# Attention over cached pages moved into the units of the forgetting attention

## The reference, cut to what matters

```python
qc, kc, vc = [t.astype(f32).reshape(B, L, H_C, HEAD_DIM) for t in jnp.split(qkv_c, 3, axis=-1)]
logf = jax.nn.log_sigmoid(f_raw.astype(f32) + P['fox_f_bias'][l].astype(f32))
if fox_past is None:            # the prompt
    k_all, v_all, lf_all = kc, vc, logf
else:                           # the samples: cached pages first, then the own 8 tokens
    k_all = jnp.concatenate([pk.astype(f32), kc], axis=1)
    v_all = jnp.concatenate([pv.astype(f32), vc], axis=1)
    lf_all = jnp.concatenate([plf.astype(f32), logf], axis=1)
d_all = jnp.cumsum(lf_all, axis=1)
# per head: s = q.k/sqrt(d) + D_t - D_s, masked to s <= t, softmax over the keys, p @ v
oc = forgetting_attention(qc, k_all, v_all, d_all[:, -L:], d_all, qpos, kpos)
```

## Time and profile before

| what | us |
|---|---|
| median of 3 runs | 1983.02 (1982.95 to 1983.48) |
| the profiled execution's own time | 1979.1 |
| its span | 1977.1 |
| forgetting attention, first to last instruction | 497.2 to 642.0 |
| attention over cached pages | 642.7 to 741.7 |
| delta rule, first instruction | 742.5 |

### The profile page before, as it was taken

One profiled execution on the slowest core, in us unless ns is written; L12 is line 12 of the kernel. 1 busy time (PEld: TensorE's weight loads), 2 busy tenths in 40 slices (PEclk: granted clock), 3 DMA queues, 4 the chain that ended last, 5 costly groups with the idle time before them and its releaser, 6 DMA issues. The chain is left out here.

```text
span 1977.1 us, 27253 instructions
## 1 busy us (share of the span) xinstructions
PE 1736.5 (88%) x10093; PEld 1499.7 (76%) x10099; DVE 857.0 (43%) x1427; ACT 572.4 (29%) x928; POOL 507.5 (26%) x710
## 2 busy tenths in 40 slices
PE   6789988999788577779869799999999998999997
PEld 2557876899565236669848599999999998778876
DVE  1451007630565223345434435555555554445444
ACT  2421132321444013222223323333333332232322
POOL 0531012220000102776303333333333332111111
PEclk6899988999899768889879899999999999999999
DMA  8325531221200217733142121111111110544443
GB/s 309 122 79 168 171 101 68 78 78 39 73 1 1 68 61 201 166 85 90 52 154 86 54 73 45 50 43 42 42 42 42 42 42 20 163 158 150 152 156 127
DMA packets 120189, 182.73 MB, mean 92 GB/s; under 512 B 31228, under 2 KB 88652, under 8 KB 116786
## 3 DMA queue, kind: packets, MB, share of 16 engines
q1 hardware_dynamic: 117650, 172.80, 27.8%
q10 hardware_dynamic: 2464, 8.91, 1.2%
HBM read 150.91 MB, written 30.65 MB: 92 GB/s over the span
## 5 line engine op out<-in xcount | busy, mean ns | idle before, releaser
L2279 PE MATMUL fu_ps<-h_hi,fu_whi 128*128 128x364 f32 (+1 forms) x1056 | 233.9, 330 | 12.4 <-ACT fu_whi L2327 12.4
L2279 PE MATMUL fu_ps<-h_lo,fu_whi 128*128 128x364 f32 (+1 forms) x1056 | 233.7, 330 | 0.0
L2279 PEld LDWEIGHTS fu_ps<-h_hi,fu_whi 128*128 128x128 f32 x1056 | 183.9, 189 | 12.5 <-ACT fu_whi L2327 12.5
L2279 PEld LDWEIGHTS fu_ps<-h_lo,fu_whi 128*128 128x128 f32 x1056 | 183.9, 189 | 0.0
L2284 PE MATMUL fu_ps<-h_hi,fu_wlo 128*128 128x364 f32 (+1 forms) x1056 | 183.1, 329 | 0.0
L2284 PEld LDWEIGHTS fu_ps<-h_hi,fu_wlo 128*128 128x128 f32 x1056 | 176.9, 188 | 0.0
L2500 PE MATMUL fd_ps<-fd_whi,fd_yhi 128*128 128x512 f32 x396 | 124.3, 395 | 19.5 <-DVE fd_wlo L2554 16.1
L2297 POOL TENSOR_TENSOR fu_wlo<-fu_w,fu_whi 128x1024 fp32r<-128x1024 f32 x44 | 117.6, 2673 | 86.1 <-ACT fu_whi L2327 86.1
L2333 ACT ACTIVATE fu_zp<-fu_ps 128x728 f32<-128x728 f32 x44 | 34.3, 779 | 356.2 <-PE fu_ps L2284 356.2
L2525 ACT ACTIVATE fd_whi<-fd_w 128x1024 fp32r<-128x1024 f32 x66 | 69.9, 1060 | 207.7 <-PE fd_ps L2500 182.9
L2500 PE MATMUL fd_ps<-fd_wlo,fd_yhi 128*128 128x512 f32 x396 | 123.7, 394 | 0.0
(11 more groups left out here) (320 smaller groups left out, 3254.0 us busy)
## 6 DMA issues: line engine op xcount, KB each, us to landing
fd_w<-in_w_down SPq DMA_DIRECT2D x66, 512.0 KB, 3.6
wa<-in_w_ada SPq DMA_DIRECT2D x24, 1024.0 KB, 7.2
fu_w<-in_w_up SPq DMA_DIRECT2D x44, 512.0 KB, 3.6
fp_w<-in_w_fm SPq DMA_DIRECT2D x16, 512.0 KB, 3.3
scr_la<-dr_la SPq DMA_DIRECT2D x16, 384.0 KB, 4.0
dr_la<-scr_la SPq DMA_DIRECT2D x16, 384.0 KB, 5.5
scr_qkv<-fp_y SPq DMA_DIRECT2D x9, 544.0 KB, 2.7
dr_stg<-scr_qkv SPq DMA_DIRECT2D x8, 576.0 KB, 6.0
```

The costliest lines, as they stand in the source:

```text
L2279: pe.matmul(ps[slot][:, n, 0:size], w_hi[:, slot, kk, :], h[:, kk, c:c + size], start=(kk == 0 and h is K.h_hi), stop=False)
```

## The change

cached_attention is gone. Its work for batch b (0 to 7) is put as three steps into forgetting_attention: step = (u - 2) % 3 with b = (u - 2) // 3 and u from 2 to 25. Step 0 is scores_c, maximum_c and exp_c, step 1 scale_c and turn_c, step 2 spread_c, values_c and decay_c of the next batch. On TensorE they stand behind all of unit u's own work. No PSUM tensor is added: the scores go to psO[1], rows 0 to 47, columns 0 to 263; the transposed probabilities to rows 0 to 63 of psO[1] and rows 64 to 127 of psO[0]; the outputs of all batches to columns 320 to 511 of the same rows, which the prompt's values leave free. They are copied out once, at the end.

Differences in what is computed: the decay is scanned on 48 partitions (each head's log-forget row is loaded to 8 partitions by a broadcast DMA) and added in maximum_c instead of by a product; only the batch's own 8 new keys are taken, not 64, and their values are loaded from scr_v; the row sums' reciprocals are applied in the transposition, as for the prompt; the values are the stationary side (64 columns for each head) and 8 columns of probabilities move, 18 products for each batch, so no mask and no picking product. GpSimd places the queries of each batch, with 6 copies. SP issues the table and pages(0) between the decay rows of pairs 0 and 1, and those of pair 2 behind pages(3). The order of TensorE, VectorE and ScalarE is in this excerpt.

```diff
+            def pages(b):
+                k, t = b % 2, SEQ + b * SSEQ
+                after(sp, ca_v, b - 1)
+                for pg in range(NPAGE):
+                    v = sp.value_load(table[0:1, b * NPAGE + pg:b * NPAGE + pg + 1], min_val=0, max_val=NPOOL - 1)
...
+                    src = K.clf[bass.ds(v, 1)].rearrange("a p n -> (a p) n").unsqueeze(1).broadcast_to([H_C, SSEQ, PAGE])
+                    sp.dma_start(dn[:, k, rows], src).then_inc(page_in[k], 16)
+                sp.dma_start(vo[:, k], K.scr_v[t:t + SSEQ]).then_inc(page_in[k], 16)
+
+            sp.dma_start(table[:], K.page_table).then_inc(table_in, 16)
+            decays(0)
+            sp.wait_ge(table_in, 16)
+            pages(0)
+            decays(1)
+            for b in range(1, NBATCH):
+                pages(b)
+                if b == 3:
+                    decays(2)
...
+            def scores_c(b):
+                pe.wait_ge(page_in[b % 2], LOADS * (b // 2 + 1))
+                pe.wait_ge(ca_q, H_C * (b + 1))
...
+                ps = psO[1][0:R]
+                for w, c in ((PAST, 0), (SSEQ, PAST)):
+                    for j in range(PAIRS):
+                        k = kp[:, b % 2, j, :] if c == 0 else K.qkc[:, PAIRS + j, SEQ + b * SSEQ:SEQ + (b + 1) * SSEQ]
+                        last = pe.matmul(ps[:, c:c + w], qb[:, b % 2, j, :], k, start=(j == 0), stop=(j == PAIRS - 1))
+                last.then_inc(ca_s, 1)
+
+            def turn_c(b):
+                pe.wait_ge(ca_dg, b + 1)
+                for c in range(2 * NPAGE):
+                    ps, rows = free[c % 2]
+                    pe.matmul(ps[rows, c // 2 * R:(c // 2 + 1) * R], pc[:, c * HD:(c + 1) * HD], dgc[:], start=True, stop=True)
+                pe.matmul(psO[1][0:SSEQ, NPAGE * R:(NPAGE + 1) * R], pc[:, PAST:KEYS], dgc[:], start=True, stop=True).then_inc(ca_t, 1)
+
+            def values_c(b):
+                pe.wait_ge(ca_pt, 3 * (b + 1))
+                for j in range(PAIRS):
+                    for c in range(NPAGE + 1):
+                        for e in range(2):
+                            h = 2 * j + e
+                            ps, rows = free[e]
+                            n = P if c < NPAGE else SSEQ
+                            v = (vp[:, b % 2, c] if c < NPAGE else vo[:, b % 2])[:, h * HD:(h + 1) * HD]
+                            o = OUT + j * NSAMP + b * SSEQ
+                            last = pe.matmul(ps[rows, o:o + SSEQ], v, ptc[0:n, c, h * SSEQ:(h + 1) * SSEQ],
+                                             start=(c == 0), stop=(c == NPAGE))
+                last.then_inc(ca_v, 1)
...
                 if u >= 3 and u % 2 == 1:
                     values((u - 3) // 2)
+                b, step = divmod(u - FIRST, 3)
+                if 0 <= b < NBATCH:
+                    (scores_c, turn_c, values_c)[step](b)
...
+            def spread_c(b):
+                act.wait_ge(ca_t, b + 1)
+                after(act, ca_v, b)
+                for ps, rows in free:
+                    act.activation(ptc[rows, 0:NPAGE], ps[rows, 0:NPAGE * R].rearrange("p (c r) -> p c r", c=NPAGE), ACT.Copy)\
+                        .then_inc(ca_pt, 1)
+                act.activation(ptc[0:SSEQ, NPAGE], psO[1][0:SSEQ, NPAGE * R:(NPAGE + 1) * R], ACT.Copy).then_inc(ca_pt, 1)
...
+                if (u - FIRST) % 3 == 2 and 0 <= (u - FIRST) // 3 < NBATCH:
+                    spread_c((u - FIRST) // 3)
                 if u >= 3 and u % 2 == 1:
                     output(act, (u - 3) // 2, 0)
                     output(act, (u - 3) // 2, 1)
+                b, step = divmod(u - FIRST, 3)
+                if step == 0 and 0 <= b < NBATCH:
+                    exp_c(b)
...
+            def decay_c(b):
+                dve.wait_ge(page_in[b % 2], LOADS * (b // 2 + 1))
+                chain.link(dve.tensor_tensor_scan(dn[:, b % 2, 0:PAST], one, dn[:, b % 2, 0:PAST], 0.0, ALU.mult, ALU.subtract))
+                dve.tensor_scalar(dn[:, b % 2, PAST:KEYS], own48[:, b], dn[:, b % 2, PAST - 1:PAST], None, ALU.add).then_inc(ca_dn, 1)
+
+            def maximum_c(b):
+                dve.wait_ge(ca_dn, b + 1)
+                dve.wait_ge(ca_s, b + 1)
+                after(dve, ca_t, b)
+                chain.link(dve.tensor_tensor_reduce(pc[:], psO[1][0:R, 0:KEYS], dn[:, b % 2], 1.0, -3e38, ALU.add, ALU.max, stc[:, 0:1]))
+                dve.tensor_scalar(stc[:, 1:2], stc[:, 0:1], -1.0, None, ALU.mult).then_inc(ca_max, 1)
+
+            def scale_c(b):
+                dve.wait_ge(ca_p, b + 1)
+                chain.link(dve.reciprocal(stc[:, 3:4], stc[:, 2:3]))
+                dve.tensor_scalar(dgc[:], K.ident[0:R, 0:R], stc[:, 3:4], None, ALU.mult).then_inc(ca_dg, 1)
...
             for u in range(UNITS + 2):
                 if u < UNITS:
                     maximum(u, 0)
                     maximum(u, 1)
+                if step == 1 and 0 <= b < NBATCH:
+                    scale_c(b)
...
+                if step == 0 and 0 <= b < NBATCH:
+                    if b == 0:
+                        decay_c(0)
+                    maximum_c(b)
+                if step == 2 and 0 <= b < NBATCH - 1:
+                    decay_c(b + 1)
```

More of the change, by code:

```diff
@@ L89, in constants @@
             r = h * SSEQ + q
[L90 to L95, removed]
+            c[r, C_CAUS:C_CAUS + SSEQ] = NEG
+            c[r, C_CAUS:C_CAUS + q + 1] = 0
     for n in range(NSEQ):
@@ L1008, in forgetting_attention @@
         nb_in = [sem("fa_nb_in0"), sem("fa_nb_in1")]
+        R = H_C * SSEQ
+        KEYS = PAST + SSEQ
+        table = sb("ca_table", [1, NBATCH * NPAGE], I32)
+        kp = sb("ca_k", [P, 2, PAIRS, PAST])
+        vp = sb("ca_v", [P, 2, NPAGE, W_C])
+        vo = sb("ca_vo", [SSEQ, 2, W_C])
+        dn = sb("ca_dn", [R, 2, KEYS])
+        qb = sb("ca_q", [P, 2, PAIRS, R])
+        pc = sb("ca_p", [R, KEYS])
+        ptc = sb("ca_pt", [P, NPAGE + 1, R])
+        stc = sb("ca_st", [R, 4])
+        dgc = sb("ca_dg", [R, R])
+        own48 = sb("ca_own48", [R, NBATCH, SSEQ])
+        (table_in, ca_clear, ca_q, own_mm, own_set, ca_dn, ca_s, ca_max, ca_p, ca_dg, ca_t, ca_pt, ca_v, ca_hi, ca_lo) = (
+            sem("ca_" + n) for n in "table_in clear q own_mm own_set dn s max p dg t pt v hi lo".split())
+        page_in = [sem("ca_page_in0"), sem("ca_page_in1")]
+        LOADS = 16 * (3 * NPAGE + 1)
+        FIRST = 2
+        OUT = 512 - PAIRS * NSAMP
         rows_of = [slice(0, HD), slice(HD, P)]
+        free = [(psO[1], rows_of[0]), (psO[0], rows_of[1])]
         groups = []
@@ L1123, in exp, with exp_c @@
                 act.activation(p, p, ACT.Exp, bias=st[:, u % 2, hh, 1:2], accum_out=st[:, u % 2, hh, 2:3]).then_inc(p_set, 1)
[L1125 to L1126 removed]
+            def exp_c(b):
+                act.wait_ge(ca_max, b + 1)
+                act.activation(pc[:], pc[:], ACT.Exp, bias=stc[:, 1:2], accum_out=stc[:, 2:3]).then_inc(ca_p, 1)
+            def spread_c(b):
[5 more added lines that the diff above has]
+                act.activation(ptc[0:SSEQ, NPAGE], psO[1][0:SSEQ, NPAGE * R:(NPAGE + 1) * R], ACT.Copy).then_inc(ca_pt, 1)
+            for u in range(UNITS + 2):
+                before = mine(u - 1, False) if 0 < u <= UNITS else []
                 half = len(before) // 2
@@ L1135, in _ @@
                     output(act, (u - 3) // 2, 1)
-            output(act, UNITS // 2 - 1, 0)
-            output(act, UNITS // 2 - 1, 1)
+                b, step = divmod(u - FIRST, 3)
+                if step == 0 and 0 <= b < NBATCH:
+                    exp_c(b)
+            act.wait_ge(ca_v, NBATCH)
+            for ps, rows in free:
+                act.activation(K.h_hi[rows, 5:8, SEQ:TOK], ps[rows, OUT:512].rearrange("p (j t) -> p j t", j=PAIRS), ACT.Copy)\
+                    .then_inc(ca_hi, 1)
         @block.vector
@@ new lines, in _ @@
+                if step == 0 and 0 <= b < NBATCH:
+                    if b == 0:
+                        decay_c(0)
+                    maximum_c(b)
+                if step == 2 and 0 <= b < NBATCH - 1:
+                    decay_c(b + 1)
+            for e, (ps, rows) in enumerate(free):
+                dve.wait_ge(ca_hi, e + 1)
+                dve.tensor_tensor(K.h_lo[rows, 5:8, SEQ:TOK], ps[rows, OUT:512].rearrange("p (j t) -> p j t", j=PAIRS),
+                                  K.h_hi[rows, 5:8, SEQ:TOK], ALU.subtract).then_inc(ca_lo, 1)
```

196 lines of the change are left out of this document (25 added, 171 removed).

## The result

The changed kernel takes 1926.2 us (median of four runs, 1925.4 to 1927.8), the kernel before 1983.3 in four runs on the same chip; the ratio is 0.971, with a 95% interval of 0.968 to 0.973. The prediction was 1930. The profiled execution took 1926.3 us with a span of 1924.2, so the span fell by 52.9 us.

The account below looks back on a forecast made before the run. Cached stage seen as short dependent chains and page loads between barriers, nothing beside it. 99.7 us removed, 47.2 added (39.6 steps, 6.5 waits, 0.8 lower clock, 0.3 start): -52.5, so 1930 us, range 1913 to 1949.

Parts of the forecast that it names:

- The removed 99.7 us: Cached attention stage, measured between last VectorE instructions of stages: its whole 99.7 us goes if nothing else moves.
- scores_c 1.75, turn_c 0.5, values_c 1.5: TensorE time per batch of the three added steps in the forgetting attention, in us at the full clock.
- Changes of form: TensorE switching stationary row counts: 0.8 us per batch inside values_c, 0.5 at step starts and inside turn_c.
- Waits added, 6.9 for values_c and 0.8 for turn_c: TensorE waiting for ScalarE's spread_c, 6.9 us over five units, and for VectorE's scale_c, 0.8 us over two.
- Waits absorbed, 1.2: Existing TensorE waits filled by scores_c before scores(21) and turn_c in unit 24: -1.2 us.
- rival D: Page loads, longer waits or lower clock partly return to TensorE's ring: 10 to 20 us more, about 1945 us; chance 0.09.
- busy time up by about 38 us: Sign to look for: TensorE's busy time in the forgetting attention rises by about 38 us.
- Put at nothing: Costs taken as zero: VectorE's additions (1.9 us per batch), ScalarE's short exponential, GpSimd's copies, SP's page loads, the tail.
- Rival C: VectorE stands in decay_c for late pages, slower than before: 2010 us at 10 us lost per batch; chance 0.03.
- Delta rule: Stage behind the removed one: clock at its start put at no change, with 5 us kept either way.
- Rival A: Added TensorE work nearly free of waits and form changes: 8 x 3.75 = 30 us, 1913 us; chance 0.10.
- Rival B: Small products dear, each values_c record 0.128 us, value-column load not overlapped: 25 us more, 1955 us; chance 0.13.

Follow-up runs that it names:

- e2: Changed kernel with every cached-attention step left out of the forgetting attention, output rows filled from queries: 1883.9 us, stage 145.7 us.
- e1: The changed kernel run again with no edit: 1923.0 us, stage 185.0 us.
- e5: Changed kernel with the batch's own 8 value rows padded with zeros to 128 in values_c: 1917.5 us, stage 178.1 us.
- e9: Changed kernel with twenty small constant products on TensorE ahead of spread_c's wait in units 4, 10, 19, 22: 1928.9 us, stage 189.2 us.
- after: The changed kernel's own profiled execution, without further edit: 1926.3 us, span 1924.2 us, stage 184.4 us.
- e3: Changed kernel with ScalarE doing spread_c at the unit's beginning, ahead of its own exponentials: 1910.8 us, stage 168.6 us.
- before: The kernel without the change, with its separate cached stage: 1983.3 us; profiled span 1977.1 us, forgetting stage 145.5 us.
- e7: Changed kernel with a batch's pages fetched only after the previous batch's values_c, not two before: 1981.9 us, stage 244.2 us.
- e6: Changed kernel with two more VectorE scans in each decay_c, three for one: 1928.2 us, stage 188.6 us.
- e10: Changed kernel with both spread_c at the unit's beginning and the 8-row chunk padded to 128: 1909.7 us, stage 166.0 us.
- e4: Changed kernel with TensorE doing the 36 records of values_c twice: 1946.3 us, stage 207.2 us.

## Why the prediction was right, and where it was not

**The forecast held** (1930; measured 1926.2), and its mechanism in outline: the cached stage gone, the price paid as TensorE work and waits inside the forgetting attention, nothing elsewhere (e2). That the number came so close is in part luck. The stage was forecast at 190 to 194 us and came out at 184.4 and 185.0: the steps and the waits were put too high, and the clock was missing. In the profiled execution the other stages were 8 us longer, in e1's 4, which hid what was left; the stages alone gained 60.9 us, not 52.5.

- *The removed 99.7 us.* Right: 99.8 by first instructions.
- *scores_c 1.75, turn_c 0.5, values_c 1.5.* Measured 1.62 to 1.66, 0.54 to 0.61, and 1.10 to 1.20 without changes of form (e5). The estimate of 0.042 us per record from the earlier trace rows was high; it is 0.031 with 8 columns moving. The Trainium skill's formula for a load (TensorE: Matmul & The Clock Gate, LDWEIGHTS) gives an estimate of 53 ns for 64 columns; taken as a pace per record, it would have been further off for values_c. The trace agrees with it where the outputs do not alternate between the halves: e9's filler passes at 0.057 us per record.
- *Changes of form.* Of the terms that were priced, the one most out of size. I priced 0.13 us from products that move 384 columns, and counted ten per batch: 1.3 us. The six inside values_c cost 0.08 each, and those at the starts of steps are already in the step lengths above. All steps together come to 3.8 to 3.9 us per batch, 31 us in all, against 39.6. The Trainium skill says that a change of tiling mode drains the engine (TensorEngine Tiling (Array Packing), Key Properties); the 0.08 us a change of e5 agree with that.
- *Waits added, 6.9 for values_c and 0.8 for turn_c.* Measured 7.4 in five waits and 1.7 in three. The two are not quite of one kind. The rule (when ScalarE is free, plus 0.6 for the copies, less the start of the next scores) gives what is added beyond any wait for VectorE that stood before those scores already, 0.68 us in unit 4. So its 2.25 stands against 2.40 - 0.68 = 1.7.
- *Waits absorbed, 1.2.* Too small, in part for that reason. TensorE's wait for VectorE before scores fell from 8.7 to 4.6 us, that for ScalarE's copies from 16.5 to 14.5. With two smaller ones it is about 7 us in after, 6 in e3. Added and absorbed together, the forecast had 6.5 us of waits and the trace 2.
- *The missing term: the clock.* Durations were taken at the full clock throughout, since it had held 1.00. It did not: about 20 us of the stage behind 518 ran at the lower level, and e3 prices it. Removing 7.4 us of waiting gained 16, so 8 to 9 us were clock and what follows from it. This is rival D's mechanism ("two or three units in which the clock falls", 10 to 20 us); it occurred in four units, a little below the low end of its price, and was outweighed by the cheaper steps and waits.
- *The balance of the stage.* TensorE is busy 37.0 us longer than before (153.1 and 116.1) and idle 1.9 us longer (31.3 and 29.4), which makes the 38.9. Of the busy time 9.6 us is the lower clock (153.1 against 143.5 in e3, the same instructions), so the steps themselves added 27.4. That is 3 to 4 us less than 8 times the length of the steps; part of it is the start of the stage, where the clock reads 0.72 in after and 0.63 in before over the first 18 us. The rest stays open. The prediction's sign "busy time up by about 38 us" thus came out by luck: the work was 27, the clock 10.
- *Put at nothing.* Pages: no wait for them in after, so the lead was enough, and e7 shows what it guards. Rival C's price was too high: it put 2010 us at 10 us lost per batch, and e7, with 10 us of waiting in each of seven batches, is level with before. Only 85% of a stall of VectorE returned, seven batches have one and not eight, and there were 60.9 us to lose, not 52.5. VectorE's additions: covered for the most part, with little room left (e6). Delta rule: its first load is issued at 684.44, 0.9 us after VectorE's last instruction (0.8 before), and TensorE is busy 12.7 of its first 20 us at a clock of 0.58, where it was 12.6 at 0.57. The table's load stands ahead of the first decay rows, not behind them; VectorE's wait for these rows was 4.2 us, and 4.9 in before, so the 0.3 put for it does not show.
- *Rival A* (steps at 3.75 us and nearly free of waits, 1913) named nearly the right cost of the steps, and e3 and e10, where the waits for spread_c are taken out, land at 1910.8 and 1909.7. *Rival B* is out by e4 and e5.

What stays open: why the clock fell behind the waits for spread_c in units 4, 10, 19 and 22 (2.40, 2.33, 1.43 and 0.86 us) and not behind waits of 1.8 us in turn, and why one fall lasts longer in one execution than in the next (after and e1). The runs show which arrangements fell; they do not isolate the rule. That the dip near 603 in e4, with no wait for spread_c, is due to the doubled small products alone was not tested apart.

## What to carry to other kernels

When work is put into the gaps of another loop, price the wait of its *last* producer first: three copies of ScalarE moved ahead of two exponentials gave 16 us of a 39 us cost (12 by the medians), while filling TensorE's other waits gave 3. After such a move, read the granted clock by stretches again, since a wait of TensorE followed by small products was paid about twice here. For a short chunk of a sum, padding the stationary side with zeros to the shape of its neighbours was cheaper here than the short product.

## What the hardware did that I had not expected

- The granted clock fell from 1.00 to 0.50 while TensorE was busy in 2.00 of 2.00 us with products of 8 moving columns (e9), and held 1.00 from 518 to 640 us (e3) and to 660 (e10) with the same steps when no wait for spread_c stood before them.
- A wait of 2.40 us, followed by values_c, cost the following scores another 1.37 us (2.93 against 1.56) in after and 0.92 in e1 (2.48).
- 36 records with 64 stationary and 8 moving columns, outputs alternating between partition halves, pass at 0.031 us each (e5); records of the same form into one half pass at 0.057 (e9). A change between a 128-row and an 8-row stationary side costs 0.08 us (e5 against after).
